# Paged stick-breaking attention: half of the sample keys turned by VectorE, half of the weight products on GpSimd

## The reference, cut to what matters

```python
def stick_breaking_block(q, k, v, bias, q_pos, k_pos):
    z = jnp.einsum('bqhd,bkhd->bhqk', q, k) * (HEAD_DIM ** -0.5) + bias[None, :, None, None]
    causal = k_pos[None, :] < q_pos[:, None]
    log_1m_beta = jnp.where(causal, jax.nn.log_sigmoid(-z), 0.0)
    tail = lax.cumsum(log_1m_beta, axis=3, reverse=True) - log_1m_beta
    w = jnp.where(causal, jnp.exp(jax.nn.log_sigmoid(z) + tail), 0.0)
    return jnp.einsum('bhqk,bkhd->bqhd', w.astype(v.dtype), v)
...
cache_k, cache_v: (DEPTH, N_PHYS_PAGES, PAGE_SIZE, N_HEADS_A, HEAD_DIM), page_table: (DEC_BATCH, N_PAGES)
```

## Time and profile before

| | us |
|---|---|
| median of 3 runs (2826.99 to 2832.66) | 2828.01 |
| the profiled execution's own time | 2821.11 |
| its span | 2819.6 |
| attention phase, 700 to 1505 us of the span | 805 |
| TensorE busy in it | 719.2 |
| VectorE busy in it | 641.4 |
| ScalarE busy in it | 596.7 |
| GpSimd busy in it | 137.6 |

### The profile page before, as it was taken

One profiled execution on the slowest core, in us unless ns is written; L12 is line 12 of the kernel. 1 busy time (PEld: TensorE's weight loads), 2 busy tenths in 40 slices (PEclk: granted clock), 3 DMA queues, 4 the chain that ended last, 5 costly groups with the idle time before them and its releaser, 6 DMA issues. The chain is left out here.

```text
span 2819.6 us, 64656 instructions
## 1 busy us (share of the span) xinstructions
PE 2586.6 (92%) x23589; PEld 1361.0 (48%) x23589; DVE 1379.9 (49%) x2816; ACT 1055.4 (37%) x1938; POOL 648.4 (23%) x918
## 2 busy tenths in 40 slices
PE   6999999996799899899998999789999998899978
PEld 3444444442455445454543555445555554555533
DVE  2151423333678788687886777522222222222228
ACT  2221314121677777687773222122222221122214
POOL 0202020101021211111111222343333333333333
PEclk9999999998899999999999999899999999999989
DMA  9011111126586766767675344399999789999947
GB/s 335 15 61 44 45 45 43 62 85 244 174 271 218 264 234 224 262 213 244 225 262 187 116 140 139 143 261 295 281 301 299 210 257 306 323 309 297 305 134 315
DMA packets 297027, 577.06 MB, mean 205 GB/s; under 512 B 80278, under 2 KB 96727, under 8 KB 292812
## 3 DMA queue, kind: packets, MB, share of 16 engines
q1 hardware_dynamic: 194472, 427.99, 47.4%
q0 software_dynamic: 102016, 146.26, 16.9%
q10 hardware_dynamic: 324, 0.10, 0.0%
HBM read 461.12 MB, written 112.29 MB: 203 GB/s over the span
## 5 line engine op out<-in xcount | busy, mean ns | idle before, releaser
L1253 DVE TENSOR_TENSOR_SCAN left<-leave,left 128x512 f32<-128x512 f32 (+3 forms) x320 | 358.4, 1120 | 134.9 <-ACT leave L1135 134.1
L442 PE MATMUL bank<-xnT,w_in 128*128 128x512 f32 x768 | 330.3, 592 | 0.0
L2056 DVE TENSOR_TENSOR sg<-sg,bank 128x128 f32<-128x128 f32 x160 | 46.0, 288 | 562.5 <-ACT sg L1992 561.3
L2023 PE MATMUL bank<-w,hT 128*32 128x256 f32 x5120 | 297.5, 380 | 1.5 <-issue 1.1
L1056 POOL DMA_DIRECT2D w_out<-in_cache_v x256 | 137.6, 538 | 660.9 <-issue 658.6
L1935 POOL DMA_DIRECT2D rowsP<-xs_d x328 | 218.0, 665 | 200.0 <-DMA rowsP<-xs_d 111.4
L2016 PE MATMUL bank<-w,o_sq 128*32 128x256 f32 x3840 | 218.0, 384 | 30.2 <-DVE o_sq L2051 23.2
L442 PEld LDWEIGHTS bank<-xnT,w_in 128*128 128x128 f32 x768 | 145.6, 190 | 181.8 <-issue 178.9
L1992 ACT ACTIVATE sg<-bank 128x128 f32<-128x128 f32 x160 | 44.4, 278 | 501.2 <-PE bank L2016 501.2
L1619 PE MATMUL bank<-w_out,w 128*128 128x512 f32 x512 | 227.7, 597 | 1.8 <-DVE w L1683 1.8
L442 PE MATMUL bank<-w_in,xnT 128*128 128x512 f32 x512 | 220.4, 592 | 0.0
(11 more groups left out here) (408 smaller groups left out, 3402.1 us busy)
## 6 DMA issues: line engine op xcount, KB each, us to landing
w_out<-in_cache_v POOLq DMA_DIRECT2D x256, 256.0 KB
w_out<-in_cache_k SPq DMA_DIRECT2D x256, 256.0 KB
w<-in_w SPq DMA_DIRECT2D x128, 512.0 KB, 17.4
w<-in_w SPq DMA_DIRECT2D x22, 2048.0 KB, 23.1
oT<-in_w SPq DMA_DIRECT2D x22, 2048.0 KB, 24.2
w_out<-in_w SPq DMA_DIRECT2D x20, 2048.0 KB, 25.7
ys_d<-zeros SPq DMA_DIRECT2D x32, 816.0 KB
ys_d<-y POOLq DMA_DIRECT2D x166, 128.0 KB, 7.8
```

The lines of the kernel that those rows point to most:

```text
L442: mm = pe.matmul(ps[:, :], w, m, start=(i == 0), stop=(i == len(parts) - 1))
L1253: dve.tensor_tensor_scan(left[n % 4][:, 0:cols][:, ::-1], leave[n % 4][:, 0:cols][:, ::-1], leave[n % 4][:, 0:cols][:, ::-1], left[n % 4][ ...
L2023: mm = pe.matmul(yb[q * Q:q * Q + Q, u * (XW // 2):(u + 1) * (XW // 2)], hT[:, u, j, :], w2[i][:, j, q * (XW // 2):(q + 1) * (XW // 2)], s ...
```

## The change

`PAGES` puts the 16 key pages of a unit in a new order, one page per tick, alternating between two groups:

- **Sequences 0 and 1 of four (TURNED = 2), 8 pages a unit.** GpSimd's queue brings the page in "strips": the access pattern `a t (s n) -> s (a t) n` spreads each token's 512 values over four groups of 32 partitions, in pieces of 128 values (512 bytes), where a page came in pieces of 2 KB. VectorE turns it with one 32x32-block transpose, 128x512, from SBUF to SBUF (`dve.transpose`). TensorE and a bank of `tb` are not used. Features and tokens then lie in another order: `keys` gives the products strided views, the queries of these sequences are laid out in that order in the phase before (a reordered copy of the projection, four more transposes and 17 more small copies), and ScalarE puts the tokens in order again with strided sigmoids, so the two sample sigmoids become four.
- **Sequences 2 and 3, 8 pages a unit.** SyncE brings them page by page; TensorE turns a page whole (still four 128x128 transposes a page) and ScalarE makes every copy.

Key pages go through 8 slots of one page. SyncE now brings all value pages too. Of the products `take` times `left`, those of odd items move to GpSimd (160 of 320). Every copy of a `turn` is ScalarE's. The copy of the last item's end goes: the scan runs over 513 columns and takes its start from the old place, with a 1 in the extra column of `leave`.

The core of the diff:

```diff
-            EVENTS.append((("turn", n - 2), "dve" if (n - 2) % 4 == 0 else "act"))
+            EVENTS.append((("turn", n - 2), "act"))
...
-        if p < 4 * FC and 0 <= unit < NU:
-            EVENTS.append((("k_turn", unit, p), "dve" if p in (3, 7, 11) else "act"))
+        if p < 4 * PPC and 0 <= unit < NU and PAGES[p][0] >= TURNED:
+            EVENTS.append((("k_turn", unit, p), "act"))
...
+    PAGES = [(j + TURNED * side, i) for j in range(TURNED) for i in range(PPC) for side in range(2)]
+    SLOTS, VALUES = 8, (4, 7, 10, 13)
...
+                def k_rows(g):
+                    u, p = divmod(g, 4 * PPC)
+                    if u < NU and PAGES[p][0] >= TURNED:
+                        dst, landed, _ = k_page(u, p)
+                        sp.dma_start(dst, cache["cache_k"][ds(page(sp, u, *PAGES[p]), 1)].rearrange("a p n -> (a p) n")).then_inc(landed, 16)
...
+                for n in range(TICKS):
+                    u, p = place(n - 1)
+                    if p < 4 * PPC and 0 <= u < NU and PAGES[p][0] >= TURNED:
+                        turned(sp, "k_turn", u, p)
+                        k_rows(4 * PPC * u + p + SLOTS)
+                    if p in VALUES and 1 <= u <= NU:
+                        v_pages(PPC * (u - 1) + VALUES.index(p) + 2)
...
+                def k_strips(g):
+                    u, p = divmod(g, 4 * PPC)
+                    if u < NU and PAGES[p][0] < TURNED:
+                        dst, landed, _ = k_page(u, p)
+                        if g >= SLOTS:
+                            pool.wait_ge(s_kd, (g - SLOTS) // 2 + 1)
+                        pool.dma_start(dst, cache["cache_k"][ds(page(pool, u, *PAGES[p]), 1)].rearrange("a t (s n) -> s (a t) n", n=P)).then_inc(landed, 16)
+
+                def weights(n):
+
+                    cols = item(n)[4]
+                    pool.wait_ge(s_tk, n + 1)
+                    pool.wait_ge(s_sc, n + 1)
+                    pool.tensor_tensor(take[n % 4][:, 0:cols], take[n % 4][:, 0:cols], left[n % 4][:, 1:cols + 1], ALU.mult).then_inc(s_wp, 1)
...
+                for n in range(TICKS):
+                    if n % 2 == 0 and 0 <= n - 1 < N:
+                        weights(n - 1)
+                    u, p = place(n - 1)
+                    if p < 4 * PPC and 0 <= u < NU:
+                        k_strips(4 * PPC * u + p + SLOTS)
...
-                    if 0 <= n - 3 < N and (n - 3) % 4:
+                    if 0 <= n - 3 < N:
                         turn(n - 3)
...
-                        dve.tensor_copy(left[n % 4][:, GRP:], left[n % 4][:, 0:1]).then_inc(s_in, 1)
+                        multiplied(n - 4)
+                        size, carry = GRP + 1, left[n % 4][:, 0:1]
...
                 def k_turn(u, p):
-                    turned(dve, "k_turn", u, p)
+                    rows, landed, count = k_page(u, p)
+                    j, i = PAGES[p]
+                    dve.wait_ge(landed, count)
                     if u:
                         turned(dve, "scores", u - 1)
-                    dve.tensor_copy(kTs[p // FC][:, p % FC, :], bank("k_turn", u, p)[:, :]).then_inc(s_cd, 1)
+                    dve.transpose(kTs[j].rearrange("p f n -> p (f n)")[:, i * GRP:i * GRP + GRP], rows).then_inc(s_kd, 1)
...
                 def turn(n):
                     cols = item(n)[4]
-                    pe.wait_ge(s_w, n + 1)
+                    pe.wait_ge(s_wp if n % 2 else s_w, n // 2 + 1)
```

More of the change, by code:

```diff
@@ L742, in _ @@
                 mm.then_inc(s["pT"], 1)
+                pe.wait_ge(s["pce"], 1)
+                for f in range(FC):
+                    mm = pe.transpose(ps["pC"][:, f * P:f * P + P], proj_c[:, f * P:f * P + P], ident[:, :])
+                mm.then_inc(s["pC"], 1)
                 modulation(0, 2, KC)
@@ L893, in attention_phase @@
         take = [k.sb(f"take{i}", [P, GRP]) for i in range(4)]
-        leave = [k.sb(f"leave{i}", [P, GRP]) for i in range(4)]
+        leave = [k.sb(f"leave{i}", [P, GRP + 1]) for i in range(4)]
         left = [k.sb(f"left{i}", [P, GRP + 1]) for i in range(4)]
@@ L947, in bank, with page, k_page, keys @@
             return tb[EVENT[name] % 3]
[L949 to L954, removed]
+        def page(eng, u, j, i):
+            at = (4 * (u // NY) + j) * NPAGES + (NY - 1 - u % NY) * PPC + i
+            return eng.value_load(pages[0:1, at:at + 1], min_val=0, max_val=NPHYS - 1)
+        def k_page(u, p):
+            g = 4 * PPC * u + p
+            return kp[g % SLOTS], s_kp[g % SLOTS], 16 * (g // SLOTS + 1)
+        def keys(j, f):
+            if j < TURNED:
+                return kTs[j].rearrange("p f n -> p (f n)").rearrange("p (b f r) -> p f b r", f=FC, r=Q)[:, f]
+            return kTs[j][:, f, :]
         with nc.Block() as block:
@@ L1227, in _ @@
                 dve.memset(left_n[:, TS:], 1.0)
+                for i in range(4):
+                    dve.memset(leave[i][:, GRP:], 1.0)
+                dve.drain()
                 first(0)
                 for n in range(TICKS + 1):
-                    if 0 <= n - 3 < N and (n - 3) % 4 == 0:
-                        turn(n - 3)
                     u, p = place(n - 1)
@@ L1249, in _ @@
                     if n < N:
[L1250 to L1254 removed]
+                        scanned(n)
                     if n == 1:
@@ L1332, in k_turn @@
                 def k_turn(u, p):
[L1333 to L1336 removed]
+                    rows, landed, count = k_page(u, p)
+                    pe.wait_ge(landed, count)
                     to = free("k_turn", u, p)
[L1338 to L1339 removed]
+                    for f in range(FC):
+                        mm = pe.transpose(to[:, f * P:f * P + P], rows[:, f * P:f * P + P], ident[:, :])
                     mm.then_inc(s_t, 1)
```

153 lines of the change are left out of this document (83 added, 70 removed).

## The result

The changed kernel takes **2936.79 us** (median of 3 runs, 2932.91 to 2942.13) against 2828.01 before: a ratio of 1.0382, 95% interval 1.035 to 1.0414. Forecast were 2781 us and a range of 2735 to 2855. It is 109 us slower, and 156 us above the forecast. The profiled execution took 2942.13 us, its span is 2940.6.

What follows compares the result with a forecast made beforehand. The prediction took the attention phase as a pipeline with TensorE longest and VectorE second. Its terms, -80 + 1 + 41 - 9 = -47 us, took the median from 2828 to 2781 us, range 2735 to 2855.

Steps and rivals of the forecast that it cites:

- the one on the queues: DMA queues, attention phase: work rises from 554 to 688 us, fits under 757 at 91%; values behind zero rows cost nothing.
- The rival of the late queue: One value or key page late by 2 us in each of 16 units: +32 us, 2813; chance 0.13; sign: `in_cache_k` waits.
- three conditions: Block transposes over 0.85 us, a strip load holding GpSimd over 2.7, or phase over 800 although TensorE is at 640.
- TensorE, -80 us: Attention phase: 512 of 1024 key transposes go, so TensorE's busy time falls by 80.0 us, 719.2 to 639.2.
- the rival without hindrance: GpSimd's products run beside VectorE's scans for free: -80 + 1 - 9 = -88 us, 2740; chance 0.20.
- close beside: ScalarE in the attention phase: 611 us of work, 655 if strided reads double sigmoids; path TensorE's or close beside it.
- Turn-taking, +41 us: VectorE's scans and GpSimd's products take turns at SBUF: even items' products 0.37 us later, 112 times, +41 us.
- The rival of one serial engine: VectorE and GpSimd work serially, at two scans in a row: phase 827 us against 805, +22, 2850; chance 0.22.
- the forecast's own sign: TensorE's turns wait for products: 94 us before, toward 140 in the forecast case, under 60 without hindrance, over 200 if serial.
- VectorE at 528 unstretched: VectorE's busy time in the attention phase: 641.4 - 200.7 + 87 = 528 us if no instruction is stretched.
- Issue of a strip load 0.95: Each of 128 strip loads takes GpSimd 0.95 us to issue, between 0.67 and 2.7; 122 us in all.
- The key waits, -9: TensorE's waits for key pages, 15.7 us on its matrix row, ease by 9 us, between 0 and 16.

Runs made afterwards that it cites:

- experiment 3: The kernel before with one change: key pages of sequences 0 and 1 come in 512-byte strips on SyncE's queue, TensorE still turning them; 3054.52 us (1.0804).

## Why the prediction was wrong

**The step that failed first is the one on the queues:** "That fits under a phase of 757 us, at 91%", and "For values behind zero rows I take nothing, since each is asked for at least six ticks ahead (15 us)". It was priced at 0; the runs give 115 us. It went wrong in three ways.
- It added engine time and compared the sum with the phase. Its price for a strip page, 1.05 us of all engines above a plain one, was too high: the 57 ns a packet are from a stretch whose packets carried 1.2 KB on the mean (1.81 MB in 1495), and the runs give 0.59 us on GpSimd's queue (75 us over 128 pages) and 0.27 on SyncE's (34 us, experiment 3). The whole was too low all the same, 688 us against 798 (0.87 of 917). And the kernel before with strips has pages up to 19.7 us late at a share of 0.58. What mattered was how long a page takes to land, which no sum of shares tells.
- It took the other queue as unaffected. SyncE's same loads occupied the engines 138 us longer beside strips (605 instead of 467), and its value pages landed in 7.8 us instead of 3.6. The longest, 18.1 us, is over any lead assumed.
- The lead of 15 us is six mean ticks. Where items are small, ticks are short, and two buffers allow no more: in the place shown 8.7 us passed from the request to the need.

The rival of the late queue had the right place and the wrong price: 2 us in each of 16 units, 32 us. The trace has 23 value waits of 3.1 us on the mean, with the rest of the coupling behind them. Its sign was looked for in the wrong place: VectorE waited 1.4 us for `in_cache_k`, so the strips, whose landing told, were in time. Late were the plain pages of the other queue, of which no row told. None of the three conditions for "the forecast is wrong" came as written: block transposes last 0.69 us, a strip load holds GpSimd 1.57, and the phase is over 800 with TensorE at 710.

**TensorE, -80 us.** The key turns' group did fall by 75 us (159.9 to 84.9), but the engine's busy time fell by 38 with plain pages and by 9 in the changed kernel. Three reasons show. Matmuls overlap: the turns (181.7), logits (164.1), key turns (159.9), values (149.9) and sample values (68.2) of before add to 723.8 us, more than the 719.2 in which anything ran, and the sample logits are not among them. So a group's row overstates what leaves with it. Other rows grew: the logits' mean went from 590 to 615 ns with plain pages. And the granted clock was lower, 0.95 with plain pages and 0.90 with strips against 0.96. The forecast took a group's busy time for the engine's.

**The path behind it.** Even without strips and without GpSimd's products the gain was 8 us, not the 88 of the rival without hindrance. In that run TensorE's busy time fell by 39 us (719.2 to 680.2), but its logits waited 44.6 us for ScalarE's `take` against 19.9 before, its turns 34.1 for VectorE's product against 25.7, and `ob` 9.4 for ScalarE's copies against 0.9. ScalarE, forecast at 611 and measured at 614 to 616, was named as "close beside" the path; it needed a price. With three engines at 78% to 86% of the phase, part of the work taken off one came back in the next hand-over.

Another part was lost behind the phase, where the forecast looked at nothing. The first products of the output projection, and the first load of their weights, in the kernel before:

```profile
1511.10 8.54 PE L1619 MATMUL bank<-w_out,xnT_s 128*32 128x512 f32 x16 [1.52 <-PEq L94]
...
1463.30 1.70 SPq L1012 DMA_DIRECT2D w_out<-in_w_out  x1
```

and in the run with plain pages and all products on VectorE:

```profile
1491.51 9.24 PE L1691 MATMUL bank<-w_out,xnT_s 128*32 128x512 f32 x16 [4.76 <-DMA w_out<-in_w_out]
1506.51 8.57 PE L1691 MATMUL bank<-w_out,xnT_s 128*32 128x512 f32 x16 [4.71 <-DMA w_out<-in_w_out]
...
1476.59 1.00 SPq L1063 DMA_DIRECT2D w_out<-in_w_out  x1
```

In these profiled executions the phase's last matmul stood at 1486.5 us, 23 us earlier than before (1509.3), but the 32 products that follow were through only 13 us earlier. SyncE, which now brings the values, reaches the load of the output weights 10 us ahead of the phase's end instead of 46. The changed kernel has the same order and pays for it too: the phase ends 109 us later than before, these products 119. No run here moves that load alone.

**Turn-taking, +41 us.** The mechanism is right: scans stretch by 47 us with plain pages and 56 with strips, only where GpSimd multiplies. Its price on the path is not shown by itself: the 4 us with plain pages are the net of that stretch and of the 89 us of products that leave VectorE (190.5 less 102.0), and VectorE had 158 us of waits for `leave` to absorb a stretch. The rival of one serial engine (+22) gave a time near the edge of the range by a mechanism that did not happen. Its sign, over 200 us of waits for products, was not seen: counted as in the prediction, the rows of weight loads and of matmuls together, they went from 94 to 164 us (61.5 + 49.5 + 37.4 + 15.9), and to 130 with plain pages, near the 140 that were the forecast's own sign. This was no confirmation, since that count adds two rows that overlap. By the matmul row alone the product ended 25.7 of TensorE's 85.8 idle us before, and not most of them as the prediction read; the logits' waits were longer (31.0).

**Small terms.** Products at 1.2 us: 1.17, together 165.8 against 165. Block transposes at 0.68: 0.69. VectorE at 528 unstretched: with all products kept there and plain pages it was busy 638.1 us, less half of their 190.5 is 543; the changed kernel has 626, and the stretch is 56 us in the scans, 6 in the samples' scans and 10 in the products (105.6 against 95.3), which leaves some 10 unexplained. Issue of a strip load 0.95: measured 1.57, within the bounds (0.67 to 2.7); its cost on the path was small, as the longest wait for GpSimd's product is 2.5 us. The key waits, -9: unchanged at 15.7 with strips, 2.7 with plain pages, so -13 had the strips not come.

What stays open: which property of the strided page makes it dear (its pieces on the memory side, or how the load is split), why strips on one queue hold up loads on the other, and how much of the clock's 0.90 is a consequence of waiting rather than a cost on its own. No tried version that computes the reference's result is faster than the kernel before by more than the noise.

## What to carry to other kernels

A free transpose by a DMA's access pattern is not free: price it by how late a page lands against its shortest lead at the place of need, in every queue that shares the engines, and not by adding engine shares. Measure it by putting the pattern alone into the old kernel, which here showed +229 us in one run (on SyncE's queue; on GpSimd's it was 115). Before paying for relief of an engine, test what the relief is worth with its costs taken away; here it was 8 us, of 23 in the phase itself. And look behind the phase: a queue with more to do also comes later to the loads of the next one.

## What was not expected of the hardware

- Loads in strips on one queue doubled the landing time of another queue's plain 256 KB pages (3.6 to 7.8 us), at a DMA share of 0.87; with 35 MB of writes taken away they landed in 9.8 us.
- The same strips cost 115 us on GpSimd's queue (in the changed kernel) and 229 on SyncE's (in the kernel before), there at a DMA share of 0.58.
- A load on GpSimd's queue with pieces of 1 KB made more packets (528 a page) than one with 512 bytes (272), the added ones of 16 and 32 bytes, and took GpSimd longer to issue: 2.11 against 1.57 us, with 0.58 for a plain page (80).
- GpSimd's products stretch VectorE's scans from 1120 to 1270 ns on the mean and a product from 0.69 to 1.62 us.
